# A two-network fp32 kernel on one core: start of the program reordered, u_hi released tile by tile at three seams, softmax scaling folded into q

## The chip, the cores and the metric

The kernel runs as one program on one core of one Trainium2 chip. The metric is the device time of a launch in microseconds; lower is better.

## The reference, cut to what matters

All arrays are fp32, 512 tokens of width 1024. A first network has two layers, a second has one:

```
for i in range(2):                                  # first network
    x = x + 0.5 * swiglu(rmsnorm(x), w_gate, w_up, w_down)         # "ffn1", width 2816
    h = rmsnorm(x) @ w_in
    y = concat(mla(h), conformer_conv(h), hyena(h))                # "mixer"; mla: 8 heads, softmax(q k^T * 96**-0.5) v
    x = x + rmsnorm_parts(y) @ w_out
    x = x + 0.5 * swiglu(rmsnorm(x), ...)                          # "ffn2"
x = rmsnorm(x)
z = rmsnorm(x) @ w_in_2                              # second network
y = gate0 * nsa(z) + gate1 * rg_lru(z) + gate2 * cross_attention(z, mem)
x = x + y @ w_o
out = rmsnorm(x + square(relu(rmsnorm(x) @ w_up)) @ w_down)        # "MLP"
```

The hyena part needs filters that come from a small sine network and tables which do not depend on x.

## The kernel before, in words

Activations lie channel-first: x, u and the others are 8 tiles (KC = 8) of 128 channels by 512 tokens. To keep fp32 accuracy with the fast matmul format, each operand is split in a high and a low part (`u_hi`, `u_lo`, `w_hi`, `w_lo`), and a product is three matmuls per chunk of 128 channels: hi·hi, lo·hi, hi·lo (L600 to L602 in `multiply`). A "unit" is one block of weights times all of u: 8 chunks, 24 matmuls of 128x512 (36 for a 12-chunk down projection), into one PSUM bank of a ring of four. SyncE's queue streams the weight blocks (512 KB for 8 chunks) into four slots `w_raw`; GpSimd (POOL) splits each block (L554 high, then L559 four quarters of low) into one of two slots, and signals `w_split`; it may split block n only when the unit n-2 is done. VectorE (DVE) and ScalarE (ACT) evict the banks, take norms and make the splits of activations.

A norm followed by a projection is folded: x is scaled by the gain, not by the root (`scaled`, L2040), ACT makes `u_hi` from it (`to_high`, L1331), DVE subtracts to give `u_lo` (`low`, L2045), and the projection starts chunk by chunk as `u_lo` arrives (`u_arrives`). Meanwhile ACT squares the tiles of x (L1363), DVE adds the squares into `std` (L2068), TensorE sums `std` over the channels by a product with ones (`square_sums`, L639), which is queued behind the first unit; ACT takes the root (L1322), DVE the reciprocal `rinv` (3.35 us), and the eviction of the projection's banks multiplies by it. `pass_over_x` is DVE's side of this, `norm_x` ACT's, `ffn` TensorE's.

At three seams the new u replaces the u that the projection before is still reading ("over operands"): the output projection of the mixer in front of ffn2, in both layers, and the `w_o` projection in front of the MLP. There DVE first evicts all eight tiles into x (L2055), one as each unit ends, with the add of the square behind each, and only after the eighth scales the first tile; ACT makes no high tile until all squares are made.

At the start, SyncE's queue issues x (2 MB), the columns of gains `cols` and the identity (L504 to L506, all counted on one semaphore), and then the weights. ACT's queue issues `rot`, the positions and everything that the filter network needs (`load_filter`, L1447 on, L1442). TensorE, ACT and DVE each wait for all three of the first loads. DVE and ACT then go tile by tile through scaled, square, high, add, low.

The mla attention (`attention`) works on 32 units of 128 queries by 512 keys in each layer. DVE takes the row maximum (L2317), waits for its own result, multiplies by minus the scale in a second instruction (L2318, a 128x1 operation) and signals ACT, which takes the exponential with that bias and the scale (L1517). DVE then inverts the sum (L2325) and normalizes (L2326), and does a piece of other work in each slot (`beside_slot`).

At the end of the second attention (`pairs`) TensorE and ACT wait until DVE has merged the last product (L2806, L2807) before ACT makes the eight high tiles of y2 (L1949), DVE the low ones (L2814), and the `w_o` projection begins.

Of the kernel before, what the change touches and what calls it, by code (L numbers as in the profile page):

```python
# [139 lines left out]
class Walk:  # L140
# [3 lines left out]
    def __init__(self):  # L144
        self.n = self.m = self.aux = self.sq = self.norm = self.full = self.split = 0
        self.tables = self.hid = self.rope = self.unit = self.part = self.item = self.vec = self.act = self.loads = self.sums = self.gate = 0
# [21 lines left out]
def build(nc, d):  # L168
# [3 lines left out]
    with ctx:  # L172
# [179 lines left out]
        u_ready = sem("u_ready")  # L352
        h_hi_ready = sem("h_hi_ready")
# [33 lines left out]
        consts_in = sem("consts_in")  # L387
        small_in = sem("small_in")
# [82 lines left out]
        def mla_units():  # L471
            return [unit(head=h, i=i, kind="plain", scale=QK ** -0.5, n=T, keep=KEEP, pt=pt,
# [30 lines left out]
        def _(sp):  # L503
            sp.dma_start(x[:, :, :], d["xt"]).then_inc(consts_in, 16)  # L504
            sp.dma_start(cols[:, :], d["cols"]).then_inc(consts_in, 16)
            sp.dma_start(ident[:, :], d["ident"]).then_inc(consts_in, 16)  # L506
            n = 0
            for k, first, count in plan:
# [14 lines left out]
                else:  # L523
                    for j in range(RING):
                        load(j)
# [59 lines left out]
        def _(pe):  # L585
# [7 lines left out]
            def multiply(n, out, k, rhs_hi, rhs_lo, i=None, ready=None, order=None):  # L593
# [3 lines left out]
                for s, c in enumerate(order or range(k)):  # L597
# [4 lines left out]
                    mm = pe.matmul(out, lo[:, c, :], rhs_hi(c), start=False, stop=(s == k - 1))  # L602
                mm.then_inc(gemm_done, 1)
# [52 lines left out]
            def looped(count, body, behind_first=None):  # L656

                for j in range(4):
                    body(j, None)
                    if j == 0 and behind_first is not None:  # L660
                        behind_first()
# [6 lines left out]
            def ffn(parts, per, steps=None, layer=0):  # L668
# [6 lines left out]
                for p, part in enumerate(parts):  # L675
# [7 lines left out]
                    for count in steps[p] if steps else (per * part,):  # L683
                        looped(count, up, behind)
# [103 lines left out]
            def pairs(units):  # L788
# [125 lines left out]
                pe.wait_ge(o_taken, w.item)  # L914
# [10 lines left out]
            def mixer(layer):  # L925
                a, m = w.small()
                out = open_bank(m)
                pe.wait_ge(f_total, layer + 1)
# [193 lines left out]
                def project(j, i):  # L1122
                    multiply(w.n + j, open_bank(w.m + j, i)[:, :], KC, lambda c: u_hi[:, c, :],
                             lambda c: u_lo[:, c, :], i)
# [7 lines left out]
            pe.wait_ge(consts_in, 16 * 3)  # L1132
# [3 lines left out]
            for layer in range(DEPTH):  # L1136
                ffn(PARTS, 2, STEPS1, layer)
# [4 lines left out]
                ffn(PARTS, 2)  # L1142
# [161 lines left out]
            def project2(j, i):  # L1304
                ready = u_arrives if i is None and j == 0 else None
                multiply(w.n + j, open_bank(w.m + j, i)[:, :], KC, lambda c: u_hi[:, c, :],
                         lambda c: u_lo[:, c, :], i, ready)

            looped(8, project2)
            ffn(PARTS2, 1)  # L1310
# [4 lines left out]
        def _(act):  # L1315
# [40 lines left out]
            def norm_x(ready, scaled_later=False, split=True, over_operands=False):  # L1356


                for c in range(KC):
# [5 lines left out]
                    if scaled_later and not over_operands:  # L1365
                        to_high(u_hi[:, c, :])
                if over_operands:
                    for c in range(KC):
                        to_high(u_hi[:, c, :])
                m = w.bank()  # L1370
# [83 lines left out]
            def filter_sines(layer, at):  # L1454

                if at == 0 and layer == 0:

# [66 lines left out]
            def pairs(units):  # L1524
# [65 lines left out]
                w.item += sum(u["closes"] for u in units)  # L1590

# [3 lines left out]
            def mixer(layer):  # L1595
# [76 lines left out]
                for hp in range(0, HEADS, 2):  # L1672
                    for dst, (a, m) in zip((k_all, q_all), at["plain"][hp:hp + 2]):
                        small_done(a)
                        act.activation(dst[0:NOPE, hp, :], ring[m % 4][0:NOPE, :], ACT.Copy)
                        take(dst[0:NOPE, hp + 1, :], ring[m % 4][NOPE:P, :], m)
# [18 lines left out]
                def beside_slot(s):  # L1695

                    if s < 6:
# [3 lines left out]
                                       ACT.Copy).then_inc(act_ready, 1)  # L1701
# [46 lines left out]
            load_filter(0)  # L1748
            act.wait_ge(consts_in, 16 * 3)
# [1251 lines left out]
```

## Time and profile before

| | us |
|---|---|
| median of 3 runs (lowest, highest) | 3167.48 (3166.11, 3168.41) |
| the profiled execution | 3168.29 |
| its span, first to last instruction | 3166.5 |
| TensorE busy in the span | 3026.3 (96%) |
| GpSimd, VectorE, ScalarE busy | 1904.3, 1630.2, 724.3 |

The profiled execution lies 0.81 us above the median; 1.79 us of it are outside the span. A busy TensorE is not one at its peak: its matmuls are pipelined. A 128x512 matmul here starts 0.227 us after the one before at full clock (2.4 GHz) and 0.427 us after it at half clock (1.2 GHz), and is shown with a duration of 0.39 or 0.63 us.

### The profile page before, as it was taken

What the parts mean: (1) busy time and instruction counts of PE and PEld (TensorE: products, weight loads), DVE (VectorE), ACT (ScalarE), POOL (GpSimd) and SP (SyncE); (2) the same over time, 40 slices, a digit from 0 to 9 for tenths busy, and PEclk for the clock granted to TensorE, in tenths of its full rate; (3) what the DMA queues carried; (4) which work ended last, traced back from release to release, by engine and by line L of the source; (5) the groups of instructions that cost most, each with busy time, mean ns of one, the idle gap of its engine ahead of it and who ended that gap; (6) DMA issues with size and microseconds to landing.
All of it is one profiled execution on the core that took longest, in us unless ns stands there. A gap on an engine that the chain in (4) does not pass through costs nothing.

```text
span 3166.5 us, 38568 instructions
## 1 busy us (share of the span) xinstructions
PE 3026.3 (96%) x14006; PEld 2353.7 (74%) x14006; DVE 1630.2 (51%) x2418; ACT 724.3 (23%) x1406; POOL 1904.3 (60%) x2079
## 2 busy tenths in 40 slices
PE   6999999989999999999988999999999999899998
PEld 5887866568888888776756788867777666678786
DVE  4424488853213532456985421366854888552524
ACT  2101012631001110111164100124332444320101
POOL 6867764037767777775412676866654333376875
PEclk9999999899999999999999999999999999999999
DMA  4323322012323222231301232323221111122322
GB/s 137 107 80 100 107 75 82 8 40 89 111 85 117 82 98 96 96 110 60 103 14 34 80 116 78 106 98 122 88 94 67 48 41 41 45 88 93 107 80 73
DMA packets 79546, 261.20 MB, mean 82 GB/s; under 512 B 16062, under 2 KB 19326, under 8 KB 78880
## 3 DMA queue, kind: packets, MB, share of 16 engines
q1 hardware_dynamic: 61344, 238.86, 22.6%
q10 hardware_dynamic: 18048, 20.27, 2.1%
q8 instruction: 99, 1.62, 0.2%
q14 instruction: 55, 0.45, 0.0%
HBM read 257.00 MB, written 2.10 MB: 82 GB/s over the span
## 4 chain that ended last, share of the span: by engine, by line
PE 84%; DVE 9%; POOL 2%; ACT 2%; issue 2%; DMA 0%; ACTq 0%; DVEq 0%; SPq 0%; POOLq 0%
PE psum L600 23%; PE psum L602 23%; PE psum L601 23%; POOL w_lo L559 2%; PE psum L827 1%; PE psum L978 1%; PE psum L843 1%; PE psum L905 1%; PE psum L847 1%; PE psum L845 1%; PE psum L750 1%; DVE mx L2373 1%; PE psum L968 1%; DVE prob L2420 1%; PE psum L874 1%
## 5 line engine op out<-in xcount | busy, mean ns | idle before, releaser
L559 POOL TENSOR_TENSOR w_lo<-w_raw,w_hi 128x256 fp32r<-128x256 f32 (+2 forms) x1644 | 1415.8, 892 | 34.3
L554 POOL TENSOR_SCALAR w_hi<-w_raw 128x1024 fp32r<-128x1024 f32 (+2 forms) x411 | 470.3, 1144 | 1139.0 <-PE psum L602 703.0
L600 PE MATMUL psum<-u_hi,w_hi 128*128 128x512 f32 x2336 | 931.1, 399 | 58.7 <-POOL w_lo L559 26.4
L602 PE MATMUL psum<-u_hi,w_lo 128*128 128x512 f32 x2336 | 915.2, 392 | 0.0
L601 PE MATMUL psum<-u_lo,w_hi 128*128 128x512 f32 x2336 | 915.0, 392 | 0.0
L600 PEld LDWEIGHTS psum<-u_hi,w_hi 128*128 128x128 f32 x2336 | 442.0, 189 | 179.1 <-issue 70.4
L601 PEld LDWEIGHTS psum<-u_lo,w_hi 128*128 128x128 f32 x2336 | 442.6, 189 | 93.1 <-issue 3.8
L602 PEld LDWEIGHTS psum<-u_hi,w_lo 128*128 128x128 f32 x2336 | 441.9, 189 | 93.9
L600 PE MATMUL psum<-h_hi,w_hi 128*128 128x512 f32 x960 | 374.7, 390 | 3.4 <-issue 3.4
L602 PE MATMUL psum<-h_hi,w_lo 128*128 128x512 f32 x960 | 373.6, 389 | 0.0
L601 PE MATMUL psum<-h_lo,w_hi 128*128 128x512 f32 x960 | 373.5, 389 | 0.0
L2172 DVE TENSOR_TENSOR htmp<-psum,rinv 128x512 f32<-128x512 f32 x88 | 60.8, 691 | 378.5 <-PE psum L602 378.5
L600 PEld LDWEIGHTS psum<-h_hi,w_hi 128*128 128x128 f32 x960 | 180.2, 188 | 46.6 <-issue 9.4
L602 PEld LDWEIGHTS psum<-h_hi,w_lo 128*128 128x128 f32 x960 | 180.2, 188 | 37.4
L601 PEld LDWEIGHTS psum<-h_lo,w_hi 128*128 128x128 f32 x960 | 180.2, 188 | 37.3
L1416 ACT ACTIVATE h_hi<-htmp 128x512 fp32r<-128x512 f32 (+1 forms) x120 | 76.0, 633 | 575.7 <-DVE htmp L2177 491.7
L2152 DVE SCALAR_TENSOR_TENSOR x<-psum,x 128x512 f32<-128x512 f32 x48 | 33.2, 692 | 329.7 <-PE psum L602 329.5
L2191 DVE TENSOR_TENSOR h_lo<-htmp,h_hi 128x512 fp32r<-128x512 f32 (+1 forms) x120 | 116.9, 975 | 107.7 <-ACT h_hi L1416 107.7
L1404 ACT ACTIVATE sg<-full 128x512 f32<-128x512 f32 x88 | 55.6, 632 | 444.4 <-DVE full L2169 444.3
L2169 DVE TENSOR_TENSOR full<-psum,rinv 128x512 f32<-128x512 f32 x88 | 60.8, 691 | 143.7 <-PE psum L602 143.5
L2055 DVE SCALAR_TENSOR_TENSOR x<-psum,x 128x512 f32<-128x512 f32 x56 | 38.7, 691 | 176.1 <-PE psum L602 165.4
L2452 DVE SCALAR_TENSOR_TENSOR tails<-conv_pad,cols,tails 128x512 f32<-128x512 f32 x120 | 116.9, 999 | 1.8
(364 smaller groups left out, 3390.2 us busy)
## 6 DMA issues: line engine op xcount, KB each, us to landing
w_raw<-in_w SPq DMA_DIRECT2D x335, 512.0 KB, 3.3
w_raw<-in_w SPq DMA_DIRECT2D x48, 768.0 KB, 4.2
w_raw<-in_w SPq DMA_DIRECT2D x32, 640.0 KB, 3.9
w_c<-in_w_c ACTq DMA_DIRECT2D x2, 2048.0 KB, 8.4
x<-in_xt SPq DMA_DIRECT2D x1, 2048.0 KB, 8.3
decay<-in_decay ACTq DMA_DIRECT2D x16, 128.0 KB, 3.7
dft<-in_dft ACTq DMA_DIRECT2D x8, 256.0 KB, 4.6
idft<-in_idft ACTq DMA_DIRECT2D x4, 512.0 KB, 5.7
```

The source lines that it names most:

```text
L554: pool.tensor_scalar(hi, raw, 1.0, 1.0, ALU.mult, ALU.mult).then_inc(w_hi_ready, 1)
L559: ins = pool.tensor_tensor(lo[:, part], raw[:, part], hi[:, part].bitcast(F32), ALU.subtract)
L600: pe.matmul(out, hi[:, c, :], rhs_hi(c), start=(s == 0), stop=False)
L601: pe.matmul(out, hi[:, c, :], rhs_lo(c), start=False, stop=False)
L602: mm = pe.matmul(out, lo[:, c, :], rhs_hi(c), start=False, stop=(s == k - 1))
L1404: act.activation(sg[c % 2][:, :], full[c % 2][:, :], ACT.Silu).then_inc(gate_ready, 1)
L1416: act.activation(dst, htmp[c % 2][:, :], ACT.Copy).then_inc(h_hi_ready, 1)
L2055: dve.scalar_tensor_tensor(tile, ring[m % 4][:, :], scale, tile, ALU.mult, ALU.add).then_inc(taken[m % 4], 1)
L2169: dve.tensor_tensor(full[c % 2][:, :], ring[gate % 4][:, :], rinv[:, :], ALU.mult).then_inc(taken[gate % 4], 1)
L2172: dve.tensor_tensor(hid, ring[up % 4][:, :], rinv[:, :], ALU.mult).then_inc(taken[up % 4], 1)
L2191: dve.tensor_tensor(dst, htmp[c % 2][:, :], high.bitcast(F32), ALU.subtract).then_inc(h_ready, 1)
L2452: ins = dve.scalar_tensor_tensor(acc, src, c("conv_w", TAPS * t + tap), acc, ALU.mult, ALU.add)
```

## The change

1. **Start.** The first weight block is issued first, then `cols`, then x in two halves of four tiles with a semaphore each; the identity goes behind the second weight block. `load_filter(0)` moves from ACT's start to just behind the first eight units of ffn1. DVE scales and splits all tiles first and adds the squares afterwards; ACT likewise makes all high tiles, then the squares.
2. **Seams.** The last unit of the projection in front signals `u_free` after each of its first seven chunks; ACT overwrites `u_hi` tile by tile on it. DVE evicts six tiles, scales three, evicts the seventh, and puts the eighth eviction between the low tiles; the last squares and adds come after the low tiles. The sums of squares are queued behind the second unit (`sums_at=1`) at these seams and at the start.
3. **mla.** The scale goes into the copies that fill `q_all`; one `tensor_reduce(..., negate=True)` replaces L2317 and L2318.
4. **End of the second attention.** TensorE's wait for the last merge stays only at the unit that takes that merge's bank (the fourth); ACT makes seven high tiles and DVE seven low tiles ahead of the last merge. The eight units of `w_o` are written out instead of looped.

```diff
@@ sync
-            sp.dma_start(x[:, :, :], d["xt"]).then_inc(consts_in, 16)
+            k0, first0, _ = plan[0]
+            sp.dma_start(w_raw[0][:, 0:k0 * P], d[f"w{k0}"][first0]).then_inc(w_loaded[0], 16)
             sp.dma_start(cols[:, :], d["cols"]).then_inc(consts_in, 16)
-            sp.dma_start(ident[:, :], d["ident"]).then_inc(consts_in, 16)
+            for h in range(2):
+                part = slice(KC // 2 * h, KC // 2 * h + KC // 2)
+                sp.dma_start(x[:, part, :], d["xt"][:, part, :]).then_inc(x_in[h], 16)
...
+                        if n + j == 1:
+                            sp.dma_start(ident[:, :], d["ident"]).then_inc(ident_in, 16)
@@ multiply (tensor)
+                    if frees and s < k - 1:
+                        mm.then_inc(u_free, 1)
@@ pairs, end (tensor)
-                pe.wait_ge(o_taken, w.item)
@@ w_o projection (tensor)
-            looped(8, project2)
-            ffn(PARTS2, 1)
+            for j in range(8):
+                out = open_bank(w.m + j)
+                if out is pair_out:
+                    pe.wait_ge(o_taken, w.item)
+                multiply(w.n + j, out[:, :], KC, lambda c: u_hi[:, c, :], lambda c: u_lo[:, c, :],
+                         ready=u_arrives if j == 0 else None, frees=j == 7)
...
+            ffn(PARTS2, 1, sums_at=1)
@@ norm_x (scalar)
+                if over_operands:
+                    for c in range(KC - 2):
+                        square(c)
+                    for c in range(KC):
+                        if c < KC - 1:
+                            act.wait_ge(u_free, w.freed + 1)
+                            w.freed += 1
                         to_high(u_hi[:, c, :])
+                    for c in range(KC - 2, KC):
+                        square(c)
+                elif highs_first:
...
@@ behind pairs (scalar)
-            act.wait_ge(o_taken, w.item)
+            wait_taken(act, m_out)
             for c in range(KC):
+                if c in (0, KC - 1):
+                    act.wait_ge(o_taken, w.item - (0 if c else 1))
@@ pass_over_x (vector)
                 if over_operands:
+                    for c in range(KC - 2):
+                        evict(c)
+                        if c:
+                            add(c - 1)
+                    for c in range(3):
+                        scaled(c)
+                    evict(KC - 2)
+                    for c in range(KC):
+                        low(c)
+                        if c == KC - 4:
+                            evict(KC - 1)
+                        if c + 3 < KC:
+                            scaled(c + 3)
+                    for c in range(KC - 3, KC):
+                        add(c)
+                elif scale is None:
                     for c in range(KC + 1):
                         if c < KC:
+                            if c % (KC // 2) == 0:
+                                dve.wait_ge(x_in[2 * c // KC], 16)
                             scaled(c)
                         if c:
                             low(c - 1)
+                    for c in range(KC):
+                        add(c)
@@ attention (vector)
-                        link(dve.tensor_reduce(mx[:, j, 0:1], sc[:, 0, 0:n], AX.X, ALU.max))
-                        dve.tensor_scalar(nb[:, j, 0:1], mx[:, j, 0:1], -u["scale"], None, ALU.mult)\
-                           .then_inc(s_max, 1)
+                        dve.tensor_reduce(nb[:, j, 0:1], sc[:, 0, 0:n], AX.X, ALU.max, negate=True).then_inc(s_max, 1)
```

## Rows read from the trace of the kernel before

**Rows 1.** The page: busy time, share of the span and instructions by engine.
```profile
PE 3026.3 (96%) x14006; PEld 2353.7 (74%) x14006; DVE 1630.2 (51%) x2418; ACT 724.3 (23%) x1406; POOL 1904.3 (60%) x2079
```

**Rows 2.** Waits of TensorE: us in total, times, longest us.
```profile
PE psum L600 <- POOL w_lo L559: 27.8, 13, 21.2
PE psum L600 <- DVE u_lo L2045: 21.8, 8, 5.9
...
PE psum L600 <- DVE u_lo L2814: 3.2, 1, 3.2
```

**Rows 3.** Timeline of the start: start us, us, engine, line, out<-in [idle before].
```profile
12.89 0.88 DVE L2040 TENSOR_SCALAR full<-x,cols 128x512 f32<-128x512 f32 x2 [11.88 <-DMA ident<-in_ident]
...
15.20 1.47 POOL L554 TENSOR_SCALAR w_hi<-w_raw 128x1024 fp32r<-128x1024 f32 x1 [14.75 <-DMA w_raw<-in_w]
...
16.75 4.17 POOL L559 TENSOR_TENSOR w_lo<-w_raw,w_hi 128x256 fp32r<-128x256 f32 x4
...
21.17 0.76 PE L600 MATMUL psum<-u_hi,w_hi 128*128 128x512 f32 x1 [21.17 <-POOL w_lo L559]
...
32.19 1.02 PE L639 MATMUL psum<-std,ones 128*128 128x512 f32 x2
...
33.65 2.83 POOL L559 TENSOR_TENSOR w_lo<-w_raw,w_hi 128x256 fp32r<-128x256 f32 x4
```

**Rows 4.** Windows of the start; the last number is GB/s moved.
```profile
1.00:10.00 9.00, 0.00 (x0) 0.00 (x0) 0.01 (x1) 1.28 (x1) 0.00 (x0) 1.00 0.93 315
```

**Rows 5.** Timeline: DVE's three operations with POOL at work, then without.
```profile
20.26 0.94 DVE L2040 TENSOR_SCALAR full<-x,cols 128x512 f32<-128x512 f32 x1
...
22.56 1.22 DVE L2045 TENSOR_TENSOR u_lo<-full,u_hi 128x512 fp32r<-128x512 f32 x1
...
24.58 1.23 DVE L2068 TENSOR_TENSOR std<-std,sq 128x512 f32<-128x512 f32 x1
...
27.86 0.68 DVE L2045 TENSOR_TENSOR u_lo<-full,u_hi 128x512 fp32r<-128x512 f32 x1
...
28.46 0.47 DVE L2040 TENSOR_SCALAR full<-x,cols 128x512 f32<-128x512 f32 x1
```

**Rows 6.** Timeline of the second seam (mixer to ffn2, layer 1).
```profile
1734.28 0.69 DVE L2055 SCALAR_TENSOR_TENSOR x<-psum,x 128x512 f32<-128x512 f32 x1 [3.73 <-PE psum L602]
...
1739.72 0.69 DVE L2055 SCALAR_TENSOR_TENSOR x<-psum,x 128x512 f32<-128x512 f32 x1 [3.73 <-PE psum L602]
...
1745.57 0.77 PE L600 MATMUL psum<-u_hi,w_hi 128*128 128x512 f32 x1 [5.89 <-DVE u_lo L2045]
...
1753.94 1.02 PE L639 MATMUL psum<-std,ones 128*128 128x512 f32 x2
```

**Rows 7.** Windows of the first unit behind that seam: PE busy, granted clock.
```profile
1745.57:1753.94 8.37, 8.37 (x24) 6.69 (x25) 6.54 (x13) 3.79 (x6) 0.00 (x0) 0.64 0.20 66
```

**Rows 8.** Timeline: end of the second attention, start of the w_o projection.
```profile
2732.32 3.68 PE L905 MATMUL psum<-pt,v 128*64 128x128 f32 x32 [0.69 <-ACT pt L1567]
2736.07 0.70 DVE L2806 SCALAR_TENSOR_TENSOR psum<-gm,psum 128x512 f32<-128x512 f32 x1 [7.60 <-PE psum L905]
...
2737.59 4.27 ACT L1949 ACTIVATE u_hi<-y 128x512 fp32r<-128x512 f32 x8 [5.32 <-DVE y L2807]
2738.32 4.91 DVE L2814 TENSOR_TENSOR u_lo<-y,u_hi 128x512 fp32r<-128x512 f32 x8 [0.83 <-ACT u_hi L1949]
2739.16 0.77 PE L600 MATMUL psum<-u_hi,w_hi 128*128 128x512 f32 x1 [3.16 <-DVE u_lo L2814]
```

**Rows 9.** Timeline of one mla slot of layer 0 on DVE.
```profile
588.34 0.69 DVE L2317 TENSOR_REDUCE mx<-psum 128x1 f32<-128x512 f32 x1
...
589.06 0.15 DVE L2318 TENSOR_SCALAR nb<-mx 128x1 f32<-128x1 f32 x1
589.13 0.15 DVE L2325 RECIPROCAL ri<-sums 128x1 f32<-128x1 f32 x1
```

**Rows 10.** ACT behind the first eight units of ffn1 (timeline).
```profile
82.71 2.55 ACT L1464 ACTIVATE sinq<-f_a 32x512 f32<-32x512 f32 x4 [8.11 <-DVE f_a L2230]
```

More of the change, by code:

```diff
@@ L387, in build @@
         consts_in = sem("consts_in")
+        ident_in = sem("ident_in")
+        x_in = [sem(f"x_in{i}") for i in range(2)]
         small_in = sem("small_in")
@@ L591, in open_bank, with multiply @@
                 return ring[m % 4]
-            def multiply(n, out, k, rhs_hi, rhs_lo, i=None, ready=None, order=None):
+            def multiply(n, out, k, rhs_hi, rhs_lo, i=None, ready=None, order=None, frees=False):
                 pe.wait_ge(w_split, at_turn(n + 1, RING, i))
@@ L1354, in norm, with norm_x, square @@
                         to_high(dst)
-            def norm_x(ready, scaled_later=False, split=True, over_operands=False):
-                for c in range(KC):
+            def norm_x(ready, scaled_later=False, split=True, over_operands=False, highs_first=False):
+                def square(c):
                     ready(c)
@@ L2077, in pass_over_x @@
                             low(c - 1)
+                    for c in range(KC):
+                        add(c)
+                else:
+                    for c in range(KC + 1):
+                        if c < KC:
+                            evict(c)
+                            if gains is not None:
+                                scaled(c)
+                        if c:
+                            add(c - 1)
+                            if gains is not None:
+                                low(c - 1)
                 if gains is not None:
@@ L2809, in _, with y2_low @@
             w.loads += 3
[L2810 to L2816 removed]
+            def y2_low(begin, end):
+                for c in range(begin, end):
+                    dve.wait_ge(u_hi_ready, w.split + 1)
+                    dve.tensor_tensor(u_lo[:, c, :], y2[:, c, :], u_hi[:, c, :].bitcast(F32),
+                                      ALU.subtract).then_inc(u_ready, 1)
+                    w.split += 1
+            pairs(nsa_units(), merge, lambda: y2_low(0, KC - 1))
+            dve.wait_ge(o_taken, w.item)
+            y2_low(KC - 1, KC)
             pass_over_x(1.0, lambda k: col("g_mlp", None, k), over_operands=True)
```

111 lines of the change are left out of this document (53 added, 58 removed).

## The prediction

> **What bounds the kernel now.** I read the page's busy times first, then TensorE's waits, then timelines of the places that those waits name. The page shows TensorE busy in 96% of the span and no other engine above 60% [rows 1]. What can be won therefore lies in the few places where TensorE stands still, or runs at half clock because it stood still. The waits name them [rows 2]: 21.2 us for the first split weights at the start, one wait; 21.8 us for `u_lo`, eight waits, of which the three longest are 5.9 us each at the three seams; 3.2 us for `u_lo` of y2. All of the change but part 3 lies there.
>
> **The start.** DVE and ACT begin at 12.89 us, when the identity, the last of three loads, has landed; POOL begins at 15.20 us, because the first weights are queued behind 2.3 MB and beside the filter loads; TensorE starts at 21.17 and the sum behind unit 0 stands at 32.19 [rows 3]. Unit 1 follows at 32.6 and unit 2 at 32.6 + 24 x 0.227 = 38.1.
>
> After: the queues moved 315 GB/s over the first 9 us [rows 4]. In the new order the first weights (0.52 MB, with `rot` and the positions, 0.26 MB, beside them) are there at about 1.0 + 0.78/0.315 = 3.5, say 4.5 with the latency; `cols` and half 0 of x at 1.0 + 2.04/0.315 = 7.5; half 1 at 10.8; the second weights at 12.5. POOL needs 1.05 + 2.83 us for a split when it is alone, 1.47 + 4.17 beside a busy DVE [rows 3], so block 0 is ready at 8.4 and no longer last. The first low tile is there at 7.5 + 0.47 + 0.63 (ACT) + 0.68, with gaps 9.4. A tile costs DVE 0.47 + 0.68 = 1.15 us alone and 0.94 + 1.22 = 2.16 beside POOL [rows 5]. Tiles 0 to 3 run alone and end at 12.5. POOL then splits block 1 until 18.1; in that time DVE does 2.6 tiles, and the last 1.4 take 1.6 us more: 19.7. Unit 0 ends a chunk later (0.68), at 20.4, unit 1 at 25.8. The eight adds now stand behind all low tiles, and POOL splits units 2 and 3 beside them: 8 x 1.23 [rows 5] = 9.8, so `std` is ready at 29.6, and TensorE waits 3.8 us behind unit 1. This is what is late next. Unit 2 starts at 30.1 instead of 38.1: 8.0 us won. A wait of that length puts the clock at risk (below); I take 1.2 us off: **6.8 us**. Bounds: if x comes only when all loads came before (12.9), everything is 5 us later, 3 us won; if POOL never disturbs DVE, unit 2 starts at 23.4, 14.7 won.
>
> The rest of this part costs nothing. Moving `load_filter(0)` puts eight DMA issues (about 5 us of ACT's queue) behind the first eight units of ffn1, ahead of the sines; there ACT idles 8.11 us for DVE's angles anyway [rows 10], and the data are wanted only eight units later. If that cover were gone it would be 5 us of ACT, of which TensorE, with four banks open, would see little. The identity is first used in the mixer.
>
> **The seams.** Take the second. The last eviction starts at 1739.72, TensorE idles 5.89 us until 1745.57, and the sum behind unit 0 stands at 1753.94 [rows 6]. Between the last matmul of the projection (its time ends at 1739.5) and that sum lie 14.4 us, for 5.44 us of work: 9.0 us lost, part of it because the unit runs at a mean granted clock of 0.64 [rows 7], that is, half clock (1.2 GHz) for 14 of its 24 matmuls.
>
> After: evictions 0 to 5 and adds are done by 1730.5, three scaled tiles by 1733.3 (0.94 each), eviction 6 at 1734.28 as now [rows 6]. The last unit starts at 1734.1, releases its first chunk at 1734.9, ACT needs 0.63, so the first low tile begins at 1735.8 instead of 1744.2. From there DVE has eight low tiles, five scaled ones and one eviction: 8 x 0.68 + 5 x 0.47 + 0.69 = 8.5 us alone. POOL is at work until about 1739.7 (the split begun at 1734.4) and from 1739.85 to 1745.3. While both work DVE does 0.53 of its own pace (1.15/2.16, rows 5), so 5.0 us of the 8.5 are done at 1745.3 and the rest at 1748.7; the unit ends at 1749.4. TensorE follows chunk by chunk from 1739.6. Won: 1753.9 - 1749.4 = 4.5 us. The three adds and two squares left come behind, by about 1752.5, and the sum, now behind unit 1, is asked for at 1754.8: no wait. The later root costs nothing either: the bank of unit 0 is wanted again by unit 4, three units (16.3 us) behind the sum; root 0.69, reciprocal 3.35 and eviction 0.69 need 5. The eighth eviction, 6.5 us later than now, frees a bank that unit 2 asks for at 1754.8. With 0.3 off for the clock, 4.2 us a seam, and the three seams show the same 5.9 us of wait: **12.6 us**. Bounds a seam: 2.0 (rival A) and 1753.9 - 1745.1 = 8.8 (TensorE never waits).
>
> The SBUF page speaks against this part. The row first: beside POOL the low tile takes 1.22 us instead of 0.68, the scaled one 0.94 instead of 0.47, and POOL's quarters 4.17 instead of 2.83 for four [rows 3, 5]. The Trainium skill, "SBUF — State Buffer", section "Who interferes with whom", says that GpSimd and such VectorE operations take one port pair in turn, as an exclusive lock for a whole instruction. By that rule the two engines' own times would add up fully. The trace shows less, and the sum above goes by the trace; the full sum is rival A.
>
> **mla.** In a slot DVE's maximum starts at 588.34, L2318 at 589.06 and the next operation at 589.13 [rows 9]: 0.79 us. Without the second instruction and the wait for its own result the next operation follows a 0.69 us one after about 0.61, so 0.17 us go, and ACT gets its bias 0.17 us earlier. L2318 stands 16 times in the chain of waits of each layer's attention: at most 2 x 16 x 0.17 = 5.4 us. TensorE's own work in a slot is near DVE's (2 us), so it becomes the bound in some: I take **4.0**, bounds 0 and 5.4. That the maximum with negation costs another time than 0.69 no row shows; I take it as equal. The scale in the copies to `q_all` rides on operations that are there.
>
> **End of the second attention.** Now TensorE's last product runs to 2736.0, then merge, high and low follow each other and the projection starts at 2739.16 [rows 8], at half clock until 2744.8, so that its first unit ends at 2747.4. After: ACT is free at 2732.3 and makes seven high tiles at 0.53 us, DVE's low ones follow at 0.61 and end at 2737.2; the merge (0.70 + 0.69) is pushed back by 1.1 us to 2738.6, the last high and low tile are there at 2740.1. TensorE starts at 2736.05 and wants chunk 7 at 2740.8 or later; its wait for the bank stands at the fourth unit, where the merge is long done. With 0 to 6 matmuls still at half clock the unit ends at 2741.5 to 2742.7: 4.7 to 5.9 won, I take **5.2**; bounds 3.2, the wait alone [rows 2], and 5.9.
>
> **Sum.** 6.8 + 12.6 + 4.0 + 5.2 = 28.6 us. All of it is on TensorE's path and nothing behind waits for a clock of its own, so it should arrive in full: 3168.29 - 28.6 = 3139.7 for the profiled execution, whose own time is 0.81 above the median of three, hence 3138.9, or 3139.
>
> **Rivals.**
> A, POOL and DVE fully in turn. For: both slow each other in rows 3 and 5. Against: a pair of them overlaps in part there. A seam then ends at 1735.8 + 8.5 + 6.9 (POOL's own work) + 0.7 = 1751.9, 2.0 won; start 4, mla 2, end 5.2: 17 us, 3151.
> B, milder contention and a clock that holds. For: POOL's splits leave gaps, and the evictions read PSUM. Start 11, seams 3 x 6.9, mla 5.4, end 5.9: 43 us, 3124.
> C, slower: TensorE's clock. Today it idles once at a seam and then works densely; afterwards unit 0 comes in bursts of 0.68 us every 2.2. If the clock falls in these and stays low behind them, each unit at half clock costs 24 x 0.2 = 4.8 us. Break-even needs 28.6/4.8 = 6 more such units over four places; nine would give +15 us, 3182. Against: at the start the unit ran in bursts too, with waits of up to 1.3 us, at full clock. The Trainium skill, "TensorE: Matmul & The Clock Gate", section "HAM oscillation — how this bites in real kernels", tells of kernels whose bursts between waits start cold each time; no run here shows that over many units.
> D, it doesn't do what it says: `std` or `u_free` comes so late that the waits only change their name. At the seams this needs DVE to be 4.5 us later than worked out, at the start 8. About 3166.
>
> **Chances.** Forecast 0.58 (own range 3132 to 3146), A 0.17, B 0.16, C 0.04, D 0.05. A change of 0.2% (6.3 us) is about what can be told from none. Faster: forecast, A and B, 0.91; same 0.05; slower 0.04. The range 3125 to 3152 takes in A and most of B.
>
> **What would show it.** First matmul near 9.5 us, third unit near 30, a wait of L639 for `std` of 3 to 4 us at the start and none at the seams. At a seam TensorE's waits for `u_lo` below 2 us each, and the sum (then behind unit 1) some 15.3 us behind the projection's end, where the one behind unit 0 stands 14.4 now. No wait behind the second attention longer than 1 us. mla stretches 2 us shorter each. Wrong would be: TensorE at half clock through a whole second unit, or waits for POOL's `w_lo` at the seams.

## The result, and the profile after

| | before | after |
|---|---|---|
| median, us | 3166.80 (3165.09 to 3168.41, 4 runs) | 3145.09 (3141.21 to 3148.11, 4 runs) |
| ratio of the two | | 0.9932, 95% interval 0.9916 to 0.9947 |
| profiled execution, us | 3168.29 | 3141.21 |
| its span, mean granted clock | 3166.5, 0.984 | 3139.4, 0.988 |

The kernel became 21.7 us faster by the medians and 27.1 us by the two profiled executions. The forecast was 28.6 us (3139); the range of all chances (3125 to 3152) held the time, and the forecast's own (3132 to 3146) held it by 0.9 us. Two questions are left: why the profiled pair shows 5 us more than the medians, and which terms of the sum were right.

In the lines after, `multiply` is L609 to L611 (L600 to L602 before), the sum L650 (L639), `low` L2092 (L2045), `scaled` L2087 (L2040), y2's low tiles L2867 (L2814).

Busy times on the page after, then TensorE's waits (us in total, times, longest); they answer to [rows 1, 2]:

```profile
PE 3023.8 (96%) x14006; PEld 2349.3 (75%) x14006; DVE 1629.1 (52%) x2354; ACT 724.3 (23%) x1406; POOL 1909.4 (61%) x2079
```

```profile
PE psum L609 <- DVE u_lo L2092: 21.8, 13, 11.8
...
PE psum L650 <- DVE std L2077: 7.8, 4, 2.4
...
PE psum L609 <- POOL w_lo L568: 5.5, 12, 1.4
...
PE psum L609 <- DVE u_lo L2867: 1.6, 1, 1.6
```

The total behind `u_lo`, 21.8 us, is what it was, and means something else: 11.8 of it is one wait at the start, which before stood as 21.2 under `w_lo`. The seams are 8.0 of it, where three waits of 5.9 became nine of 0.76 to 1.05; two more waits at the start and one at a norm that the change doesn't touch are the rest. A total over all places hides that; only the longest and the count tell it.

The start after (timeline), to hold against [rows 3]:

```profile
4.58 1.05 POOL L563 TENSOR_SCALAR w_hi<-w_raw 128x1024 fp32r<-128x1024 f32 x1 [4.12 <-DMA w_raw<-in_w]
5.70 2.77 POOL L568 TENSOR_TENSOR w_lo<-w_raw,w_hi 128x256 fp32r<-128x256 f32 x4
8.39 0.88 DVE L2087 TENSOR_SCALAR full<-x,cols 128x512 f32<-128x512 f32 x2 [7.38 <-DMA x<-in_xt]
8.96 1.28 ACT L1344 ACT_TABLE_LOAD   x1 [8.96 <-DVE full L2087]
10.26 1.15 ACT L1344 ACTIVATE u_hi<-full 128x512 fp32r<-128x512 f32 x2
10.92 0.69 DVE L2092 TENSOR_TENSOR u_lo<-full,u_hi 128x512 fp32r<-128x512 f32 x1 [1.65 <-ACT u_hi L1344]
...
11.76 0.77 PE L609 MATMUL psum<-u_hi,w_hi 128*128 128x512 f32 x1 [11.76 <-DVE u_lo L2092]
...
21.64 7.52 DVE L2077 TENSOR_TENSOR std<-std,sq 128x512 f32<-128x512 f32 x7
...
29.22 1.12 PE L650 MATMUL psum<-std,ones 128*128 128x512 f32 x2 [0.96 <-DVE std L2077]
```

Block 0 is split at 8.47 (forecast 8.4). Then a load of ScalarE's function table, 1.28 us, stands between the first scaled tile and the first high one. It was in the old trace too, at 6.66, beside the wait for x; now it comes behind that wait.

The third seam after (timeline of DVE, then of TensorE):

```profile
2757.74 0.69 DVE L2065 SCALAR_TENSOR_TENSOR x<-psum,x 128x512 f32<-128x512 f32 x1 [1.04 <-PE psum L611]
2759.16 1.14 DVE L2092 TENSOR_TENSOR u_lo<-full,u_hi 128x512 fp32r<-128x512 f32 x1 [0.72 <-ACT u_hi L1344]
...
2770.99 3.02 DVE L2077 TENSOR_TENSOR std<-std,sq 128x512 f32<-128x512 f32 x3
```

```profile
2766.19 0.50 PE L609 MATMUL psum<-u_hi,w_hi 128*128 128x512 f32 x1 [0.86 <-DVE u_lo L2092]
...
2768.20 0.50 PE L609 MATMUL psum<-u_hi,w_hi 128*128 128x512 f32 x1 [1.05 <-DVE u_lo L2092]
...
2769.92 0.50 PE L609 MATMUL psum<-u_hi,w_hi 128*128 128x512 f32 x1 [0.76 <-DVE u_lo L2092]
...
2777.54 1.02 PE L650 MATMUL psum<-std,ones 128*128 128x512 f32 x2
```

The first low tile is made 1.4 us behind the seventh eviction, and TensorE waits 0.86, 1.05 and 0.76 us where it waited 5.89 at once [rows 6]. The sum, now behind unit 1, waits for nothing.

The granted clock in the 20 us that end with the sum, at each of the three seams (stretch, PE busy, clock, DMA, GB/s); first before, then after:

```profile
693.17:713.17 20.00, 14.11 (x51) 0.83 0.24 79
1733.94:1753.94 20.00, 14.11 (x50) 0.83 0.24 80
2779.26:2799.26 20.00, 14.11 (x54) 0.83 0.23 79
```

```profile
682.17:702.17 20.00, 17.34 (x66) 0.91 0.22 72
1719.30:1739.30 20.00, 17.34 (x62) 0.83 0.20 66
2757.54:2777.54 20.00, 17.33 (x73) 1.00 0.24 80
```

These rows carry most of what follows. 0.83 over 20 us is 3.4 us lost at half clock (1.2 GHz), 0.91 is 1.8, 1.00 (2.4 GHz) nothing. One execution has all three values, behind the same three short waits (0.86, 1.04 or 1.05, and 0.76 us at each seam).

The end of the second attention after, against [rows 8], and an mla slot after, against [rows 9]:

```profile
2712.36 3.68 PE L916 MATMUL psum<-pt,v 128*64 128x128 f32 x32 [0.69 <-ACT pt L1596]
2716.11 3.75 ACT L1980 ACTIVATE u_hi<-y 128x512 fp32r<-128x512 f32 x7 [3.81 <-PE psum L916]
2716.78 4.30 DVE L2867 TENSOR_TENSOR u_lo<-y,u_hi 128x512 fp32r<-128x512 f32 x7 [8.38 <-ACT u_hi L1980]
...
2717.61 0.77 PE L609 MATMUL psum<-u_hi,w_hi 128*128 128x512 f32 x1 [1.57 <-DVE u_lo L2867]
...
2721.00 0.69 DVE L2860 SCALAR_TENSOR_TENSOR psum<-gm,psum 128x512 f32<-128x512 f32 x1
```

```profile
577.79 0.69 DVE L2370 TENSOR_REDUCE nb<-psum 128x1 f32<-128x512 f32 x1
578.39 0.16 DVE L2376 RECIPROCAL ri<-sums 128x1 f32<-128x1 f32 x1
```

ACT's high tiles were to start at the product's start, beside it. They start at its end: ACT waits 3.81 us for L916. In the mla slot the next operation follows 0.60 us behind the maximum instead of 0.79, as worked out; the maximum with negation takes the same 0.69.

Starts of four sums in the trace say where the time went:

| | before | after | won in the stretch |
|---|---|---|---|
| first norm of mixer 0 | 402.92 | 394.62 | 8.3: start |
| first norm of layer 1's mixer | 1445.39 | 1428.95 | 8.1: mla 3.6, seam 1 3.5, 1.0 other, with the clock |
| norms behind layer 1 | 2111.28 | 2091.21 | 3.6: seam 2 2.5, mla nothing, 1.1 other, with the clock |
| last norm | 3153.17 | 3126.17 | 6.9: end of attention 2.6, seam 3 4.6, 0.3 lost elsewhere |

### The profile page after: what moved, and what is told of

It reads as the page before. It is cut to its first block and busy times, and to the rows that moved or that the text cites. A ratio compares the mean times of both kernels' runs of the same rounds, so it can differ in the third digit from the quotient of the medians.

```text
span 3139.4 us, 38528 instructions
## 1 busy us (share of the span) xinstructions
PE 3023.8 (96%) x14006; PEld 2349.3 (75%) x14006; DVE 1629.1 (52%) x2354; ACT 724.3 (23%) x1406; POOL 1909.4 (61%) x2079
## 5 line engine op out<-in xcount | busy, mean ns | idle before, releaser
L609 PE MATMUL psum<-u_hi,w_hi 128*128 128x512 f32 x2336 | 931.2, 399 | 36.3 <-DVE u_lo L2092 21.8
L611 PE MATMUL psum<-u_hi,w_lo 128*128 128x512 f32 x2336 | 914.6, 392 | 0.0
L609 PEld LDWEIGHTS psum<-u_hi,w_hi 128*128 128x128 f32 x2336 | 441.2, 189 | 162.9 <-issue 40.5
L611 PEld LDWEIGHTS psum<-u_hi,w_lo 128*128 128x128 f32 x2336 | 441.5, 189 | 93.5
L609 PE MATMUL psum<-h_hi,w_hi 128*128 128x512 f32 x960 | 374.8, 390 | 3.6 <-issue 3.6
L611 PE MATMUL psum<-h_hi,w_lo 128*128 128x512 f32 x960 | 373.6, 389 | 0.0
L609 PEld LDWEIGHTS psum<-h_hi,w_hi 128*128 128x128 f32 x960 | 180.2, 188 | 46.8 <-issue 9.6
L611 PEld LDWEIGHTS psum<-h_hi,w_lo 128*128 128x128 f32 x960 | 180.2, 188 | 37.7
```

The lines of the kernel that those rows point to most:

```text
L609: pe.matmul(out, hi[:, c, :], rhs_hi(c), start=(s == 0), stop=False)
```

## The experiments

Four kernels have one part of the change each, put on the kernel before.

**Start alone.**

```diff
-            sp.dma_start(x[:, :, :], d["xt"]).then_inc(consts_in, 16)
+            sp.dma_start(w_raw[0][:, 0:k0 * P], d[f"w{k0}"][first0]).then_inc(w_loaded[0], 16)
...
-            load_filter(0)
+                    load_filter(0)          # behind the first eight units of ffn1
```

> The start alone on the kernel before (weights first, x in two parts, identity and filter tables later, high and low tiles ahead of squares and adds, sum behind unit 1 in the first ffn). Theory, clocks read from the trace of after: the third unit starts at 29.8 us instead of 38.1, and all of it stays: 8 us less than before. Rival, that part of it is given back at the mixer or eaten by the filter loads: 5 us or less.

3159.58 us (3157.40 to 3160.58, 11 runs), ratio 0.9974 [0.9965, 0.9983]: 7.6 less than the 3167.16 of the kernel before in these runs. The start is worth what was forecast before the 1.2 us off for the clock. Its profile has that loss too: a wait of 2.39 us for `std` and then 0.91 in the stretch from 20 to 40 us, so that only 5.3 us are won by the mixer's first norm.

**Seams alone.**

```diff
-                    for c in range(KC):
-                        square(c)
-                    for c in range(KC):
-                        to_high(u_hi[:, c, :])
+                    # squares 0-5, then each high tile on u_free, then squares 6, 7
...
-                ffn(PARTS, 2)
+                ffn(PARTS, 2, sums_at=1)
```

> The three seams alone (u_free, new orders of DVE and ACT, sum behind unit 1). Theory: 4.6 us a seam where TensorE stays at full clock in unit 0, 2 to 3 where it falls to half clock in it, so 7 to 14 us less than before, and a spread between runs of more than the 3 us that the kernel before has. Rival, the spread of after comes from elsewhere: 13 to 14 us less, as steady as before.

3153.46 us (3152.74 to 3155.68, 5 runs), 0.9958 [0.9945, 0.9972]: 13.7 less. The spread is 2.9 us: size and spread are those of the rival. Clock at the three seams:

```profile
691.86:711.86 20.00, 17.33 (x74) 1.00 0.22 79
1726.05:1746.05 20.00, 17.34 (x73) 1.00 0.25 80
2769.84:2789.84 20.00, 17.34 (x67) 0.91 0.19 65
```

From the first matmul of the projection to the sum, at the first two seams, it is 59.1 us in both with unit 1 inside, against 58.7 and 59.0 without it before: 5.2 us won a seam at full clock, since unit 1 is 24 x 0.227 = 5.4. Three things were changed together here (the release of `u_hi` by tile, the order on DVE and ACT, the place of the sum); only the last was taken back alone (below).

**mla alone.**

```diff
-                        link(dve.tensor_reduce(mx[:, j, 0:1], sc[:, 0, 0:n], AX.X, ALU.max))
-                        dve.tensor_scalar(nb[:, j, 0:1], mx[:, j, 0:1], -u["scale"], None, ALU.mult)
+                        dve.tensor_reduce(nb[:, j, 0:1], sc[:, 0, 0:n], AX.X, ALU.max, negate=True)
```

> The folded scale and the negated maximum alone. Theory as predicted: 4 us less than before (bounds 0 and 5.4). Rival, from the traces (layer 0 3.6 us shorter, layer 1 none): that the slots gain but the clock at the waits decides, 0 to 2 us less.

3163.03 us (3158.06 to 3166.96, 11 runs), 0.9987 [0.9978, 0.9996]: 4.1 less, with the widest spread of all. From the first score to the first matmul of `w_out` the layers take 94.5 and 94.1 us against 96.9 and 94.7. The kernel before is a poor measure here, since its own two layers differ by 2.2. The start alone leaves the attention as it was; its stretches, then those of mla alone (stretch, PE busy, clock, DMA, GB/s):

```profile
551.62:646.81 95.19, 85.80 (x503) 0.92 0.02 6
1592.70:1687.88 95.18, 85.79 (x503) 0.92 0.02 6
```

```profile
556.57:651.09 94.52, 86.78 (x502) 0.92 0.02 6
1594.84:1688.92 94.08, 86.35 (x503) 0.92 0.02 6
```

At the same clock the edit is worth about 0.9 us a layer. Over all profiles, eight such stretches without the edit take 94.5 to 96.9 us, mean 95.3, and twenty with it 93.3 to 94.8, mean 94.2: 1.1 us a layer, 2.2 in all. The rest of the 4.1 lies outside the attention's stretches, and the interval of this ratio (1.3 to 7.0 us) holds 2.2 too.

**End of the second attention alone.**

```diff
-            pairs(nsa_units(), merge, lambda: None)
+            pairs(nsa_units(), merge, lambda: y2_low(0, KC - 1))
...
-            act.wait_ge(o_taken, w.item)
             for c in range(KC):
+                if c in (0, KC - 1):
+                    act.wait_ge(o_taken, w.item - (0 if c else 1))
```

> The end of the second attention alone. Theory: ACT still waits for TensorE's last product inside pairs (its high tiles start at 2716.1, when the product ends), so only the merge leaves the path: 1.6 us of wait and about 0.7 of slow matmuls, 2.3 us less than before. Rival, the prediction's 5.2 us.

3165.57 us (3162.41 to 3166.53, 11 runs), 0.9993 [0.9984, 1.0002]: 1.6 less, not told from nothing by its interval, and far from 5.2. The place itself shows more: from the start of the last product to the end of the projection's first unit it is 12.6 us against 15.1 before, 2.5 won, as the theory had it.

The four alone add to 27.0 us, the whole gave 21.7. The next runs ask where the 5 us are.

**The changed kernel again, unaltered.**

```diff
(no edit; its lines stand one further down)
```

> The changed kernel once more, nothing altered. Theory A (the four edits are worth 27 us when the clock is the same, and the missing 5 us of the median are clock falls inside the seams that come in some executions and not in others): times spread over 5 us or more, 3139 to 3148, and a shorter execution shows a higher granted clock in the two seam stretches. Rival (the edits get in each other's way by a fixed amount): the times lie together near 3145 with a spread under 3 us.

3145.99 us (3144.19 to 3147.60, 5 runs), 0.9935 [0.9921, 0.9948]. The spread, 3.4 us, is nearer to the rival's. But the profiled execution, 3.0 us longer than the first, agrees with it within 0.3 us at the start (sum at 29.26) and in the last 1000 us; it differs by 2.7 us between the norms at 394.6 and 1431.6, and 0.6 more before 2094.4. Its seams:

```profile
684.82:704.82 20.00, 17.42 (x61) 0.83 0.20 62
1722.53:1742.53 20.00, 17.48 (x62) 0.83 0.20 62
2760.69:2780.69 20.00, 17.32 (x73) 1.00 0.23 80
```

0.17, 0.17 and 0 of 20 us are 6.8 us lost; with the seams alone 0, 0 and 0.09, 1.8 us. The difference has the size of the missing 5 us. Three later kernels that change nothing at seams 1 and 2 (ScalarE's idle wait, the table load, GpSimd's second split) show 0.83 at both too, so the whole change seems to meet them at half clock more often than the seams alone do.

That this is the whole cause is not shown. The profiles of the four parts, measured to the last norm, win 31.6 us together, the second profile of the whole 24.0. Up to the mixer's first norm the whole wins 3.1 us more than the parts together, between there and the norms behind layer 1 it wins 14.6 less (8.5 against 23.1), behind them 4.0 more. The start alone and the end alone edit nothing between those norms, and are 2.0 and 1.0 us shorter there than the kernel before. So the missing 5 us are a balance of differences of the same size in places that weren't edited.

**ScalarE's idle wait.** In the pipeline's last step ACT waits for a product whose bank nothing needs then.

```diff
-                    if s >= 2:
+                    if 2 <= s <= steps:
                         act.wait_ge(pv_done, u0 + 2 * s - 2)
```

> The changed kernel with one edit: in the last step of the attention's pipeline ScalarE no longer waits for the last product's matmuls (pv_done) ahead of the epilogue's high parts, since nothing is issued in that step that needs the bank. Theory (the step 'end of the second attention' gave 2.3 us where 5.2 was forecast because this wait holds ScalarE's high parts): TensorE's wait on the first u_lo tile after the product goes from 1.6 us to about 0, the merge starts right behind the product, and the kernel is 2 to 3 us shorter than the changed kernel in the same session, near 3142. Rival (the high parts are held by their own producer, and the wait in the code is idle): no change, within 0.5 us.

3143.67 us (3143.38 to 3146.10, 5 runs), 0.9929 [0.9915, 0.9942]. The ranges of the two overlap, so the times alone don't show 2.3 us. The timeline does:

```profile
2715.43 3.74 ACT L1980 ACTIVATE u_hi<-y 128x512 fp32r<-128x512 f32 x7
2715.58 3.28 PEld L916 LDWEIGHTS psum<-pt,v 128*64 128x64 f32 x32 [1.05 <-ACT pt L1596]
2715.58 3.68 PE L916 MATMUL psum<-pt,v 128*64 128x128 f32 x32 [0.69 <-ACT pt L1596]
...
2719.20 0.80 PE L609 MATMUL psum<-u_hi,w_hi 128*128 128x512 f32 x1
```

The high tiles now run beside the product, and the projection starts 3.6 us behind the product's start instead of 5.2, without a wait. From the product to the last high tile of the third seam it is 54.6 us against 56.9. Of these 2.3 us 1.6 are the wait, and 0.7 is less of the first unit at half clock. The theory holds.

**The table load ahead of x as well.**

```diff
+            act.wait_ge(vec_ready, 1)
+            act.activation(e0[:, 0, 0:1], ones[:, 0:1], ACT.Square)
             act.wait_ge(consts_in, 16)
```

> As fix_end, and ScalarE makes one Square of one column right behind the start's ones, before it waits for x, so that the function table is loaded while x is still on its way. Theory (the table load of 1.28 us behind x's arrival delays the first high tile and all of unit 0 by as much): the first matmul begins about 1.3 us earlier than in the changed kernel, near 10.5 us, and the kernel is 1.0 to 1.3 us shorter than fix_end. Rival (the first low tile from VectorE or the split of w_0's low part ends last, and the load was beside it): first matmul within 0.3 us of before and no difference to fix_end.

3144.52 us (3143.24 to 3146.59, 5 runs), 0.9931 [0.9917, 0.9944]: nothing more. Against the second profile of the changed kernel the first matmul begins at 10.69 us, 1.13 earlier, and the sum at 29.00, only 0.26 earlier: TensorE's wait for `std` grew from 1.1 to 2.4 us. GpSimd splits block 1 from 12.35 to 17.5, as before, and DVE's low tiles beside it take 1.22 us. The Trainium skill, "ScalarE: Activation LUTs", section "What ACT_TABLE_LOAD costs", gives 1.283 us for the load and about 2.7 with a drain; at the start here the high tile begins right behind the 1.28.

**Filled waits.** Three extra matmuls, their result unused, ahead of chunks 3, 4 and 5 of unit 0. The expectation says "at the start and the three seams", but the edit reaches the seams only, since the first ffn has `steps` and `hold` is false there. The page counts 27 extra matmuls, 9 at each of three places.

```diff
+                    if hold and s in (3, 4, 5):
+                        for _ in range(3):
+                            pe.matmul(banks[5][:, :], hi[:, s - 1, :], rhs_hi(s - 1), start=True, stop=True)
                     if ready is not None:
                         ready(s)
...
+                                 hold=steps is None and ready is not None)
```

> The changed kernel with three extra matmuls ahead of each of the chunks 3, 4 and 5 of unit 0 at the places that wait for u_lo tiles (their result is not used), at the start and the three seams. Each such wait was 0.7 to 1.0 us; three matmuls at full clock last 0.68 us, so they lie nearly inside the wait. Theory (the waits of unit 0 let the clock fall to half for 1.7 and 2.8 us' worth of work at two seams): with the waits filled the granted clock stays at 1.00 in both seam stretches, and the kernel is 2 to 5 us shorter than the changed kernel, with a smaller spread. Rival 1 (what draws the clock down is what ran ahead of the seam, not these waits): clock as in the changed kernel, time longer by up to 12 x 0.1 us = 1 us. Rival 2 (extra work pushes the tiles back): 2 to 6 us longer.

3149.50 us (3147.92 to 3151.20, 5 runs), 0.9942 [0.9929, 0.9956]: 3.5 slower than the changed kernel, in the range of rival 2 but not for its reason. Its profile at two seams, then near 2270, and the same stretch of the changed kernel:

```profile
684.75:704.75 20.00, 19.41 (x82) 1.00 0.23 79
1719.13:1739.13 20.00, 19.38 (x83) 1.00 0.25 79
...
2262.00:2292.00 30.00, 27.37 (x152) 0.69 0.29 93
```

```profile
2262.00:2292.00 30.00, 26.92 (x188) 1.00 0.33 110
```

At the seams the clock stays up, as the theory had it (1.00 at the third too), and the stretches from a mixer's first norm to the sum of its seam are 2.9 and 3.3 us shorter than in the second profile of the changed kernel. But near 2270, at the weights of the memory, it waits 1.4 us for `w_lo` as the changed kernel does, and then falls to half clock for 20 us: 10 us given back, where nothing had been edited. The time of arrival alone isn't the reason: the norms behind layer 1 stand at 2091.03 here and at 2091.21 in the changed kernel's first profile, which doesn't fall.

**Filled waits at the first two seams only.**

```diff
+                                 hold=ready is not None and steps is None and per == 2)
```

> The changed kernel with three extra matmuls (their result is not used) ahead of chunks 3, 4 and 5 of unit 0 at the first two seams only, not at the start and the third seam. With them everywhere, the stretch up to the sum behind the first seam's unit 1 was 2.9 us shorter than in the changed kernel and that of the second 3.3 us shorter, at a granted clock of 1.00, but 20 us at half clock came near 2270 in the last phase, 10 us. Theory A (the fall near 2270 hangs on how the start is timed or on the third seam): it stays away, and the kernel is 5 to 6 us shorter than the changed kernel, near 3140. Theory B (the clock answers to when the work of the last phase comes, which 6 us less ahead of it shift as before): the two seams gain 6 us and the fall near 2270 takes up to 10 back, 3143 to 3150.

3151.25 us (3139.08 to 3152.89, 6 runs), 0.9944 [0.9932, 0.9957]: five within 2.3 us of each other and one 12 us faster. The profiled one, at 3152.89, has 1.00 at both seams, the fall near 2270, and 0.83 at the third seam. With 18 extra matmuls it differs from the run before at the third seam alone, so of theory A only that part was tested. Five of six runs speak for theory B, 1 us above its range in the median; the sixth has theory A's time. The fast one has no profile; that it escaped these falls fits the 13 us that they cost, but wasn't seen.

**Sums behind unit 0 at the seams.**

```diff
-                ffn(PARTS, 2, sums_at=1)
+                ffn(PARTS, 2)
...
-            ffn(PARTS2, 1, sums_at=1)
+            ffn(PARTS2, 1)
```

> The changed kernel with the sums of squares put back behind unit 0 at the three seams (as before the change); the low tiles still come first and the adds after them. In the profile of the changed kernel std of the third seam is ready at 2774.0, and unit 0 has ended near 2770.8. Theory (the release by tile makes unit 0 early, but the adds now come last, so it pays only with the sums behind unit 1): TensorE waits about 3.2 us for std at each seam and the kernel is 7 to 10 us slower than the changed kernel, near 3154. Rival (the adds are ready by the end of unit 0, the move of the sums is idle): within 1 us of the changed kernel.

3147.38 us (3146.53 to 3149.90, 5 runs), 0.9940 [0.9928, 0.9953], 1.4 above the changed kernel, not 7 to 10. A wait for `std` shows at the third seam alone:

```profile
2779.37 1.10 PE L650 MATMUL psum<-std,ones 128*128 128x512 f32 x2 [1.89 <-DVE std L2077]
```

My expectation had unit 0 end at 2770.8; its last chunk can't start before the last low tile (2771.1) and it ended near 2772.1. At seams 1 and 2 it runs at half clock and ends after `std` is there. So the theory was wrong in size: the move of the sums saves 0 to 1.9 us, and the gain at the seams comes from the release by tile and the new orders of DVE and ACT, which weren't separated.

**GpSimd's second split behind the low tiles** (with the table load ahead of x).

```diff
+                    if m == 1 and i is None:
+                        pool.wait_ge(u_ready, KC)
                     pool.wait_ge(w_loaded[m % RING], at_turn(16 * (m // RING + 1), 16, i))
```

> The changed kernel with two edits at the start: ScalarE's table load ahead of its wait for x (as in the run before, where it brought the first matmul 1.1 us forward and unit 2 nothing), and GpSimd's split of the second weight block only behind the eighth low tile. Theory (what ends last at the start is VectorE's chain of low tiles and adds beside GpSimd's splits: 1.22 us for a low tile beside one and 0.68 without): the low tiles end near 18 instead of 21 us, the sums of squares near 27 instead of 29.3, and the kernel is about 2 us shorter than the changed kernel, near 3143.5. Rival (the second weight block is then what comes last: its low part is ready only 4 us behind the low tiles, and the third and fourth are as much later): TensorE waits 2 to 3 us for w_lo at unit 1 and again at unit 2, and the kernel is the same or up to 2 us longer.

3139.64 us by the median, 0.9920 [0.9907, 0.9933], but in two groups: 3139.41, 3139.42, 3139.64 and 3145.58, 3146.95. The profile is of the upper one and shows the rival at work:

```profile
23.06 0.80 PE L611 MATMUL psum<-u_hi,w_hi 128*128 128x512 f32 x1 [4.37 <-POOL w_lo L570]
```

The low tiles end at 17.2 instead of 21.2, unit 0 with them, and TensorE then waits 4.37 us for block 1. The sum stands at 29.98, 0.7 later than in the changed kernel. The start is not better.

**The three corrections together**: ScalarE's idle wait gone, the table load ahead of x, GpSimd's second split behind the low tiles.

```diff
-                    if s >= 2:
+                    if 2 <= s <= steps:
...
+            act.activation(e0[:, 0, 0:1], ones[:, 0:1], ACT.Square)
...
+                        pool.wait_ge(u_ready, KC)
```

> The edits of the runs fix_end and pool_wait together in the changed kernel: ScalarE's idle wait in the attention's last step gone, the table load ahead of x, GpSimd's second split behind the low tiles. Theory (fix_end is worth 2.2 us in its stretch; the two start edits exchange one wait for another, within 1 us; pool_wait's three times at 3139.4 to 3139.6 and two at 3145.6 and 3147.0 are one kernel at two levels of the clock in its last 1000 us): in the profile the sum at the start stands within 1 us of the changed kernel's 29.3, the stretch from the last product of the attention to the last high tile of the third seam is 54 to 55 us against 56.9, and the times fall in two groups about 6 us apart, near 3137 and 3144. Rival (the start edits are worth 6 us, and the slower two were disturbed): all five near 3137, and the stretches ahead of 400 us shorter by several us.

3137.10 us (3135.62, 3137.03, 3137.10 and 3142.21, 3143.04), 0.9913 [0.9900, 0.9927]: the lowest of all, in two groups 5 to 6 us apart, as the theory had it. The profiled execution is of the lower group. The stretch from the product to the last high tile is 54.2 us. At the start the sum stands at 31.41, 2.1 later than in the changed kernel, where the theory had it within 1 us. What makes it fast are the seams:

```profile
684.65:704.65 20.00, 17.36 (x73) 1.00 0.23 79
1718.92:1738.92 20.00, 17.79 (x69) 0.91 0.22 77
2752.90:2772.90 20.00, 17.31 (x73) 1.00 0.25 81
```

They lose 1.8 us where those of the changed kernel's second profile lost 6.8. Two small edits at the start, worth less than nothing where they are, seem to have changed how the rest meets the clock; two of five executions lie 6 us higher. That the upper group has its falls at the seams wasn't profiled here; the upper profile of the run before has them (0.83, 0.83, 1.00).

## Why the prediction was right or wrong

**Start, 6.8 forecast.** 8.3 in the profiled pair, 7.6 alone. Unit 2 began at 29.78 (30.1 forecast), by errors that cancelled, which is luck. x came 0.9 us later than worked out, the table load took 1.28 and unit 0 ran at half clock until 21, so that it ended near 22.9 instead of 20.4. But the adds took 7.9 us, not 9.8: the first of the eight is a copy of 0.42 us and not an add of 1.23, and GpSimd stood idle for a free buffer until 22.99, so that about two of the others ran alone (0.68 us each without GpSimd). TensorE's wait for `std`, forecast as 3.8, was 1.0 (2.4 in other runs). The table load was a missing step: I read it as hidden and didn't ask what it would stand behind. It costs next to nothing after all, 0.26 us at the sum, as its removal showed.

**Seams, 3 x 4.2.** The queue of tiles was right: 4.6 us at the third seam, at full clock, against 4.5 worked out. What failed is "with 0.3 off for the clock". Of the first two seams of the changed kernel one lost 1.8 and one 3.4 us to half clock, and in its second profile both lost 3.4; at 0.83 a seam wins 2.5 us (61.8 against 58.9 + 5.4), at full clock 5.2. Of the rivals, C had the mechanism (bursts of three matmuls between short waits draw the clock down) at less than a sixth of its price (6.8 us for 43): the clock is back within 1 us of the unit's end. The filled waits speak for it: five filled seams in two profiles stand at 1.00, and the one that the second of these kernels leaves unfilled at 0.83. The Trainium skill, "TensorE: Matmul & The Clock Gate", section "A second HAM failure mode: psum-queue depth-cycling", tells of a kernel in which short idles between groups of matmuls make the clock go to and fro between its two levels. The trace after agrees at the first two seams (0.91 and 0.83), with waits of 0.76 to 1.04 us. A fall is not certain, though: the third seam has the same waits and 1.00, and with the seams alone the first two have it as well, unfilled. What decides between them stays open.

**Rival A**, the full lock between DVE and GpSimd, would have given 2.0 us a seam. 4.6 at full clock speaks against it, as did [rows 5].

**mla, 4.0.** 4.1 alone; in the profiled pair 3.6 in layer 0 and nothing in layer 1. The instruction saved 0.19 us in each slot, as worked out. How much arrives differs between layers and executions by more than its size; at equal clock and over all profiles it is about 1 us a layer, so the term was some twice too large, and the agreement of the totals is luck.

**End of the second attention, 5.2.** 2.6, and 1.6 alone by the medians (2.5 in its stretch): here a step failed. "ACT is free at 2732.3 and makes seven high tiles" was false: ACT's program has a wait for the last product ahead of them (`pv_done`, at every step from the second on). I moved the work and didn't read what stands in front of it on its queue. With that wait gone, 2.3 us more came: from the product's start to the end of the projection's first unit it is 15.1 us before, 12.5 after, 10.2 with the wait gone, 4.9 in all, inside the forecast's 4.7 to 5.9. The rest of the step came as worked out.

**The sum.** 28.6 forecast, 27.1 in the profiled pair, 24.1 to the second profile, 21.7 by the medians. The first profile was the fastest of its four executions. The second lies 4.5 us short of the forecast. The attention's step makes 2.6 of it, the seams 3.0 (9.6 won at the three, with the clock at two of them), mla 0.9 as measured against the kernel before; the start gave 1.5 more than forecast, and 0.5 came elsewhere. The other 2.4 us between the two profiles and the medians (1.5 before, 0.9 after) no trace explains.

Of the signs, the third unit, the seams without a wait for `std` or `w_lo` and the waits for `u_lo` below 2 us came. The sum stands 14.4 us behind the projection's end at full clock and 17.1 at 0.83, for 15.3. Missed were the first matmul (11.76 us for 9.5), the wait for `std` at the start (1.0 for 3 to 4), the wait behind the second attention (1.57, not below 1) and the mla stretches (1 us shorter each, not 2).

## What to carry to other kernels

Before a moved step is costed, read every wait that stands ahead of it on its engine, those that the trace doesn't show because they are satisfied today too. Splitting one long stall into short ones can keep the clock's loss although the stall is gone: compare the granted clock stretch by stretch, and price the gain at both levels. And where a kernel has places that fall to half clock in some executions and not in others, a median of five can move 6 us with no cause at the place of the edit: compare stretches of two profiles between common marks, and believe an edit by its own stretch.

## What the hardware showed that was not expected

- With 9 extra matmuls (2 us) at each of three seams the clock at seams 1 and 2 was 1.00 where it had been 0.83, and the clock fell 530 us behind the second of them for 20 us (0.69 over 30 us against 1.00), where code and wait (1.4 us) were those of the changed kernel. It came again with the extra matmuls at the first two seams only. Why stays open.
- The times of three of these programs come in groups (those of the changed kernel itself don't): 3139.4 to 3139.6 and 3145.6 to 3147.0; 3139.1 and 3150.7 to 3152.9; 3135.6 to 3137.1 and 3142.2 to 3143.0. Within a group they agree to 2.3 us or better.
- A load of ScalarE's function table sits here ahead of a wait on a DMA or behind it, depending on which activation comes first and what it waits for: at 6.66 us before, hidden, at 8.96 after, in the path.
